# Two buffers for the residual rows h, their norm made at the change of tiles, and the sample tile's loads put in another order

## The reference, cut to what matters

```
proj = rmsnorm(x, norm_mix_w) @ w_in
mix  = concat(window_attention(proj), hgrn2(proj)) @ w_o
h    = x + mix
hn   = h * rsqrt(mean(h*h) + eps) * norm_ffn_w
qry  = hn @ w_q ; sc = qry . sub_keys          # 8 heads x 2 x 128 scores
eidx, gate = top-16 of the 16x16 sums of the two top-16 lists, per head
act  = gelu(peer_u[eidx] . hn)                 # 128 rows of 1024 per token
y    = rmsnorm(h + sum_k gate*act * peer_v[eidx], norm_final_w)
```

## Time and profile before

| what | value |
|---|---|
| time, median of 3 runs | 3365.28 us (3364.44 to 3366.7) |
| the profiled execution | 3362.58 us |
| its span, first to last instruction | 3360.8 us |
| PE, PEld busy | 2938.7 us (87%), 1386.4 us (41%) |
| DVE, ACT, POOL busy | 2104.9 us (63%), 1533.5 us (46%), 2069.1 us (62%) |
| bytes moved by DMA | 1222.63 MB, mean 364 GB/s |
| copies of L1585 (changes of tiles), us | 267.5, 665.8, 1051.4, 1422.6, 1791.1, 2147.1, 2498.4, 2847.1 |
| change to the sample tile's picks (L1582) | 3262.0 us |

### The profile page before, as it was taken

How to read it: one execution, slowest core, us unless ns; L and a number is a source line. 1 busy time by engine, 2 the same in 40 slices (tenths; PEclk the granted TensorE clock), 3 DMA queues, 4 the chain that set the end, 5 groups by cost and what they waited for, 6 DMA issues and landing times.

```text
span 3360.8 us, 31493 instructions
## 1 busy us (share of the span) xinstructions
PE 2938.7 (87%) x8213; PEld 1386.4 (41%) x8213; DVE 2104.9 (63%) x4852; ACT 1533.5 (46%) x4160; POOL 2069.1 (62%) x2162
## 2 busy tenths in 40 slices
PE   8997999979987999789987898789978997689976
PEld 6853544435443444335433443244333442244221
DVE  2465556756575656766585758665776668354694
ACT  3414643357334653367334743475346533263333
POOL 1105565666656666676667766776677667464675
PEclk9998999999999999899999999999989998798999
DMA  8419999999989999999999999999999999899998
GB/s 295 159 51 353 361 386 347 378 410 404 396 319 400 408 390 366 369 410 404 393 329 403 409 410 388 374 409 410 397 361 410 409 404 355 316 379 335 355 353 343
DMA packets 358876, 1222.63 MB, mean 364 GB/s; under 512 B 42747, under 2 KB 65244, under 8 KB 357404
## 3 DMA queue, kind: packets, MB, share of 16 engines
q0 software_dynamic: 308288, 1121.46, 86.0%
q1 hardware_dynamic: 22540, 66.55, 5.3%
q10 hardware_dynamic: 27872, 32.61, 2.9%
HBM read 1195.69 MB, written 25.79 MB: 363 GB/s over the span
## 4 chain that ended last, share of the span: by engine, by line
PE 47%; DMA 17%; DVE 15%; POOL 7%; issue 7%; ACT 6%; SPq 0%; ACTq 0%; DVEq 0%; POOLq 0%
PE ps L1123 24%; DMA rows<-in_peer_v,idx 11%; PE ps L1005 7%; DMA rows<-in_peer_u,idx 6%; PE ps L874 5%; DVE rows L1540 5%; POOL rows L483 4%; PE ps L988 4%; POOL rows L493 4%; PE ps L836 2%; DVE r L1421 1%; DVE r L1422 1%; DVE r L1386 1%; DVE r L1425 1%; DVE r L1381 1%
## 5 line engine op out<-in xcount | busy, mean ns | idle before, releaser
L1123 PE MATMUL ps<-rows,diag 128*128 128x512 f32 (+1 forms) x4224 | 2037.8, 619 | 333.8 <-DMA rows<-in_peer_v,idx 175.3
L1540 DVE CUSTOM_DVE_ANT_0 rows<-rows,ps 128x1024 f32<-128x1024 f32 x1056 | 1261.1, 1217 | 631.2 <-DMA rows<-in_peer_u,idx 628.5
L493 POOL DMA_INDIRECT rows<-in_peer_v,idx x1056 | 1025.7, 971 | 594.0 <-PE ps L1123 376.1
L483 POOL DMA_INDIRECT rows<-in_peer_u,idx x1056 | 1018.4, 964 | 577.7 <-issue 258.9
L1123 PEld LDWEIGHTS ps<-rows,diag 128*128 128x128 f32 (+1 forms) x4224 | 778.0, 193 | 1435.5 <-issue 1114.4
L760 ACT ACTIVATE act_g<-act_g 128x1 f32<-128x1 f32 x1056 | 210.9, 200 | 1070.8 <-DVE act_g L1540 1057.5
L766 ACT ACTIVATE diag<-ident,act_g 128x128 f32<-128x128 f32 x1024 | 411.3, 402 | 400.4 <-PE ps L1123 374.7
L762 ACT ACTIVATE act_g<-act_g,gate 128x1 f32<-128x1 f32 x1056 | 311.0, 295 | 34.3
L1005 PE MATMUL ps<-w_sc,r 128*128 128x512 f32 (+1 forms) x576 | 280.1, 595 | 1.7 <-ACT r L676 1.7
L874 PE MATMUL ps<-rows 128*128 128x416 f32 (+1 forms) x704 | 243.7, 501 | 0.0
L874 PEld LDWEIGHTS ps<-rows 128*128 128x128 f32 x704 | 134.3, 191 | 108.7 <-issue 67.9
(11 more groups left out here) (283 smaller groups left out, 1829.5 us busy)
## 6 DMA issues: line engine op xcount, KB each, us to landing
rows<-in_w_in ACTq DMA_DIRECT2D x42, 512.0 KB, 6.6
rows<-in_peer_u,idx POOLq DMA_INDIRECT x1056, 8.5
rows<-in_peer_v,idx POOLq DMA_INDIRECT x1056, 8.4
r<-proj SPq DMA_DIRECT2D x7, 1344.0 KB, 11.5
proj<-staged ACTq DMA_DIRECT2D x44, 192.0 KB, 7.2
w_sc<-in_w_q_t SPq DMA_DIRECT2D x8, 1024.0 KB, 8.8
rows<-in_w_in POOLq DMA_DIRECT2D x14, 512.0 KB, 3.9
w_o<-in_w_in POOLq DMA_DIRECT2D x10, 512.0 KB, 6.9
```

The lines of the kernel that those rows point to most:

```text
L483: nc.gpsimd.indirect_dma_start(ring[:, slot, :], None, a["peer_u"], bass.IndirectOffsetOnAxis(ap=idx[g % 2][:, k:k + 1], axis=0), engine_s ...
L493: nc.gpsimd.indirect_dma_start(ring[:, slot, :], None, a["peer_v"], bass.IndirectOffsetOnAxis(ap=idx[g % 2][:, k:k + 1], axis=0), engine_s ...
L1123: last = nc.tensor.matmul(Y[j][0:m, :], diag[:, n % DIAGS, 0:m], ring[:, slot, 512 * j:512 * (j + 1)], start=(k == 0), stop=(k == steps_of ...
L1540: V.tensor_tensor_reduce(ring[:, slot, :], ring[:, slot, :], hn_u, 1.0, 0.0, ALU.mult, ALU.add, col).then_inc(S["dots"], 1)
```

## The change

`hx` and `hn` are replaced by `resid[0]` and `resid[1]`; tile t keeps its h in `resid[t % 2]` until its y is stored from there. The DRAM copy of h and its loads are gone.

The front no longer makes `hn`. PE transposes h itself at q = 86. At q = 87 DVE multiplies the transposed rows by `norm_ffn` (a column per partition, `w_ffn_t`, loaded once at the start with elements of 4 bytes) and makes the reciprocal root. ACT applies the root as a scale of its copy of the scores. At the change of tiles, one DVE instruction writes h * rstd * norm_ffn into `hn_u`. For it, `norm_ffn` is loaded into the first half of `r2` as soon as the candidates there are dead (`cand_done`, q = 126), and `norm_final` into the second half at the same time; before, it was loaded after `topk_done`.

Of the sample tile's loads, the copies of the caches between DRAM tensors go to the start of the program, the two cache loads to the period before (after `mix_attn` of tile 7), and `proj_s`, `s_mask`, `s_onehot` and two stores ahead of the y store of tile 6. Only the keys `k_t` (now before the store of `k_win_prompt`) and x_sample stay behind it.

```diff
-        hn = sb("hn", [P, D])
-        hx = sb("hx", [P, D])
+        resid = [sb(f"resid{n}", [P, D]) for n in range(2)]
...
+            sp.dma_start(w_ffn_t, a["norm_ffn"][0, :].rearrange("(c p) -> p c", p=P), allow_slow_non_contiguous=True).then_inc(S["consts_in"], 16)
...
             def load_sample(f):
 
+                sp.dma_start(spj, proj_s[:, 0:CHUNKS - 1, :]).then_inc(S["proj_in"], 16)
+                sp.dma_start(s_mask, a["s_mask"]).then_inc(S["caches_in"], 16)
+                sp.dma_start(s_oh, a["s_onehot"]).then_inc(S["caches_in"], 16)
                 sp.dma_start(a["v_win_prompt"], v_n[:, 1, :]).then_inc(S["out_kv"], 16)
                 sp.dma_start(a["state_prompt"], state[:, :, :]).then_inc(S["out_kv"], 16)
+
+            def load_sample_k(f):
+
                 sp.wait_ge(S["k7_kept"], 1)
+                sp.dma_start(k_t[:, 1, 0:NS], proj_s[:, CHUNKS - 1, :]).then_inc(S["proj_in"], 16)
                 sp.dma_start(a["k_win_prompt"], r3[:, 896:1024]).then_inc(S["out_kv"], 16)
...
                 if f is not None:
                     load_front(f)
+                    if is_sample(f):
+                        load_sample(f)
                     finish(w)
                     if is_sample(f):
-                        load_sample(f)
-                    if f:
-                        sp.wait_ge(S["hn_ready"], f)
-                    sp.dma_start(hx[0:ntok(f), :], a["x_sample"] if is_sample(f) else x_tiles[f]).then_inc(S["x_in"], 16)
+                        load_sample_k(f)
+                    sp.dma_start(resid[f % 2][0:ntok(f), :], a["x_sample"] if is_sample(f) else x_tiles[f]).then_inc(S["x_in"], 16)
+                    if f == TILES - 1:
+                        sp.wait_ge(S["mix_attn"], f + 1)
+                        load_caches()
                     if is_sample(f):
                         sample_caches(f)
-                    sp.wait_ge(S["h_ready"], f + 1)
-                    h_at = h_dram[SEQ:TOK, :] if is_sample(f) else h_tiles[f]
-                    sp.dma_start(h_at, hx[0:ntok(f), :]).then_inc(S["h_stored"], 16)
-                    sp.wait_ge(S["h_stored"], 16 * f + 16)
+                    sp.wait_ge(S["cand_done"], f + 1)
+                    sp.dma_start(w_ffn, a["norm_ffn"]).then_inc(S["w_ffn_in"], 16)
+                    sp.dma_start(w_fin, a["norm_final"]).then_inc(S["w_fin_in"], 16)
...
                         act.wait_ge(S["sc_mm"], 4 * f + g + 1)
+                        act.wait_ge(S["rstd_ready"], f + 1)
                         nc.scalar.activation(sc[0:n, 4 * g:4 * g + 4, :], F[SCORE_BANK[g]][0:n, :].rearrange("p (c t) -> p c t", c=4),
-                                             ACT.Copy).then_inc(S["sc_kept"], 1)
+                                             ACT.Copy, scale=rstd[0:n, :]).then_inc(S["sc_kept"], 1)
...
                 if q == 87:
+                    dve.wait_ge(S["h_turned"], f + 1)
...
+                    for j in range(2):
+                        last = V.tensor_tensor(hn_t[:, 4 * j:4 * j + 4, 0:n],
+                                               F[j][:, 0:4 * n].rearrange("p (c t) -> p c t", c=4),
+                                               w_ffn_t[:, 4 * j:4 * j + 4].unsqueeze(2).to_broadcast([P, 4, n]), ALU.mult)
+                    last.then_inc(S["h_t_kept"], 1)
                     dve.wait_ge(S["ssq_root"], f + 1)
-                    dve.wait_ge(S["w_ffn_in"], 16 * f + 16)
-                    mark(V.reciprocal(rstd[0:n, :], rstd[0:n, :]))
-                    settle()
-                    V.scalar_tensor_tensor(hn[0:n, :], hx[0:n, :], rstd[0:n, :], hn[0:n, :], ALU.mult, ALU.mult)\
-                        .then_inc(S["hn_ready"], 1)
-                    dve.wait_ge(S["hn_ready"], f + 1)
+                    V.reciprocal(rstd[0:n, :], rstd[0:n, :]).then_inc(S["rstd_ready"], 1)
...
                     else:
-                        V.tensor_copy(hn_u, hn[:, :]).then_inc(S["hn_taken"], 1)
-                        dve.wait_ge(S["hn_taken"], f + 1)
+                        mark(V.scalar_tensor_tensor(hn_u, resid[f % 2][:, :], rstd, w_ffn, ALU.mult, ALU.mult))
+                    settle()
```

More of the change, by code:

```diff
@@ L68 @@
 S_OFF = (C_G + 4 - 1) * NS
+S_NEXT = S_OFF + D + NS
 PASS1 = 2 * P
@@ L197, in build @@
         idx = [sb(f"idx{n}", [P, PICKS], I32) for n in range(2)]
-        small = sb("small", [P, 192])
+        small = sb("small", [P, 200])
         ps = ctx.enter_context(nc.psum_tensor("ps", [P, 8, 512], F32))
@@ L212, in build @@
         w_mix = vec(DC)
+        w_ffn_t = vec(DC)
         mix_scale = vec(DC)
@@ L223, in build @@
         staged_s = vec(NS)
-        assert taken[0] <= 192
+        assert taken[0] <= 200
         names = """consts_in w_o_in w_q_in x_a0 x_a1 masks_in masks_kept a_root a_scaled a_turned a_kept w_a0 w_a1 w_a2 w_a3 w_b0 w_b1
@@ L283, in build @@
                     5: (xn_first, 0), 6: (xn_first, P), 7: (xn_first, 2 * P)}
-        table = hn[0:BUCKETS + 1, :].rearrange("p (h q) -> p h q", h=HEADS)
-        bucket_of = hx[0:BUCKETS + 1, 0:SKEW]
+        table = resid[1][0:BUCKETS + 1, :].rearrange("p (h q) -> p h q", h=HEADS)
+        bucket_of = resid[0][0:BUCKETS + 1, 0:SKEW]
         replicated = [r2[:, 0:4 * SKEW], bias[:, 0:4 * SKEW]]
-        w_fin = r2[:, D:2 * D]
+        w_ffn, w_fin = r2[:, 0:D], r2[:, D:2 * D]
         kc_t = bias[:, 0:D]
@@ L295, in build @@
         s_probs_t = [r2[:, D + NS + c * P:D + NS + (c + 1) * P] if c < 7 else
[L296 to L300, removed]
+                     r1[:, S_NEXT + 652 + (c - 7) * P:S_NEXT + 652 + (c - 6) * P] for c in range(9)]
+        s_mask = r1[:, S_OFF:S_NEXT]
+        s_bias = r1[:, S_NEXT:S_NEXT + 264].rearrange("p (g j) -> p g j", g=KV)
+        s_oh = r1[:, S_NEXT + 264:S_NEXT + 396]
+        s_tab = r1[:, S_NEXT + 396:S_NEXT + 652]
         s_nat = r1[0:NS, S_OFF:S_OFF + D]
@@ L370, in finish @@
                     sp.wait_ge(S["y_ready"], w + 1)
-                    sp.dma_start(a["y_sample"] if is_sample(w) else y_tiles[w], hx[0:ntok(w), :]).then_inc(S["y_out"], 16)
+                    sp.dma_start(a["y_sample"] if is_sample(w) else y_tiles[w], resid[w % 2][0:ntok(w), :]).then_inc(S["y_out"], 16)
                     sp.wait_ge(S["y_out"], 16 * w + 16)
@@ L411, in load_sample @@
                 sp.dma_start(vc, a["cache_v"].rearrange("b j x -> j b x")).then_inc(S["caches_in"], 16)
[L412 to L416, removed]
             def sample_caches(f):
@@ L440, in sample_caches @@
                     sp.wait_ge(S[f"st_out{b % 3}"], 16 * (b // 3 + 1))
+            for out_name, in_name in (("k_win_sample", "cache_k"), ("v_win_sample", "cache_v")):
+                sp.dma_start(a[out_name][:, 0:WINDOW - DEC_T, :], a[in_name][:, DEC_T:WINDOW, :])\
+                  .then_inc(S["cache_out"], 16)
             for p in periods:
@@ L666, in front @@
                     act.wait_ge(S["h_ready"], f + 1)
-                    own.mark(nc.scalar.activation(r2[0:n, 0:D], hx[0:n, :], ACT.Square, accum_out=ssq[0:n, :]))
+                    own.mark(nc.scalar.activation(r2[0:n, 0:D], resid[f % 2][0:n, :], ACT.Square, accum_out=ssq[0:n, :]))
                     own.settle()
@@ L670, in front @@
                       .then_inc(S["ssq_root"], 1)
[L671 to L678, removed]
                 for g in range(4):
@@ L793, in _ @@
                         act.wait_ge(S["y_taken"], w + 1)
-                        own.mark(nc.scalar.activation(r2[0:m, 0:D], hx[0:m, :], ACT.Square, accum_out=ssq_y[0:m, :]))
+                        own.mark(nc.scalar.activation(r2[0:m, 0:D], resid[w % 2][0:m, :], ACT.Square, accum_out=ssq_y[0:m, :]))
                         own.settle()
@@ L991, in front @@
                         last.then_inc(S["h_mm"], 1)
-                if q == 88:
-                    pe.wait_ge(S["hn_ready"], f + 1)
-                    turn(F[0], hn[:, 0:512], 4, n)
-                    turn(F[1], hn[:, 512:1024], 4, n).then_inc(S["hn_turned"], 1)
+                if q == 86:
+                    pe.wait_ge(S["h_ready"], f + 1)
+                    turn(F[0], resid[f % 2][:, 0:512], 4, n)
+                    turn(F[1], resid[f % 2][:, 512:1024], 4, n).then_inc(S["h_turned"], 1)
                 if 90 <= q < 114:
@@ L1372, in front @@
                     settle()
+                    dve.wait_ge(S["cand_done"], f + 1)
                     for j in range(2):
```

56 lines of the change are left out of this document (22 added, 34 removed).

## The result

| what | before | after |
|---|---|---|
| median of the runs on one chip, us | 3365.91 (4 runs) | 3330.36 (4 runs, 3324.65 to 3335.46) |
| the profiled execution, us | 3362.58 | 3335.46 |
| its span, us | 3360.8 | 3333.7 |
| bytes moved by DMA | 1222.63 MB | 1214.90 MB |
| changes of tiles, us | (table above) | 265.9, 664.1, 1046.7, 1416.3, 1781.2, 2132.8, 2481.5, 2834.05; sample 3237.16 |

The ratio is 0.9894, 95% interval 0.9877 to 0.9912: faster, by 35.6 us in the medians and by 27.1 us from one profile to the other. The forecast was 3338 us, range 3318 to 3354.

The account below looks back on a forecast made before the run. DMA bounds the first and last stages, PE the projection and scores, DVE the top-16 stage; a chain of waits delays the sample tile. Terms sum to -27.3 us, from the median 3365.28 to 3338 us, range 3318 to 3354.

Parts of the forecast that it names:

- Sample stall: Start of the sample tile: only the keys stay behind the y store, so PE gets on at 2875.8, -16.3 us.
- Rival 4: Start of the sample tile: another late thing ends PE's wait, so the -16.3 goes; 3354 us, chance 0.08.
- Sample and cache loads moved: Loads moved into DMA-bound places: sample loads and stores at topk_done of tile 7 +3.1 us, cache loads in period 6 +2.6.
- The norms at `cand_done`: norm_ffn and norm_final leave DMA-bound places for the stage where DVE is the limit: -15 us, bounds 0 and -17.9.
- rival 1: Only the sample tile gains; bytes moved to cand_done cost there what they saved; 3353 us, chance 0.17.
- rival 3: At cand_done the burst of two loads starves DVE of u rows, +41 us; 3379 us, chance 0.05.
- h out and back: h's store and load, 17.9 us of traffic in the stage where PE is full: valued at 0, bounds 0 and -17.9.
- rival 2: Every byte counts, h's 1 MB beside the full PE too; 3317 us, chance 0.15.
- Transpose two picks earlier: PE before the scores gains 0.25 us a tile, -2 us for 8 tiles, bounds 0 and -7.
- The change of tiles: One DVE instruction of 1285 ns replaces a copy of 1228 ns: +0.7 us, with rounding +1.
- Tile 0: Norm of tile 0, which nothing covers: scores start near 188.6 instead of 190.31, -1.7 us, bounds 0 and -5.
- The start: Load of w_ffn_t, 1,024 elements of 4 bytes, may land late for DVE: +1 us, bounds 0 and +6.

Follow-up runs that it names:

- The whole reordering: Changed kernel with the sample tile's loads and the copies between DRAM tensors put back in their old place: 3337.86 us, 7.4 us above the changed kernel.
- the repeat: The changed kernel run again with no edit, giving its second profile: median 3330.48 us, ratio 0.9896, profiled execution 3331.51 us.
- the kernel with late norms: Changed kernel with norm_ffn and norm_final loaded at topk_done instead of cand_done: 3352.6 us, ratio 0.9968, 22.1 us above the changed kernel.
- the added stores: Changed kernel plus 14 stores of 512 KB behind the keys, at h_ready or at cand_done: 3506.02, 3505.29, 3504.64 us on the third chip, changed kernel 3492.15.
- With the keys early: Changed kernel with the sample tile's keys loaded ahead of the y store of tile 6: 3316.41 us, ratio 0.9861, 14.1 us under the changed kernel.

## Why the prediction was right

The mechanism held for the two large terms. The sum of -27.3 us was made against the profiled execution, and from that to the profiled one after it is -27.1; that these agree to 0.2 us is luck. The medians differ by 35.6, as the profiled run of before was faster than its other runs and that of after the slowest of its four, and the second profile of the changed kernel is 31.1 under the one before. Term by term:

- *Sample stall, -16.3.* PE's wait ends 16.0 us sooner, by the chain that was forecast. But `h_ready` of the sample tile comes only 11.4 us sooner behind the change (245.9 against 257.3), and period 7 is 11.9 us shorter (403.1 against 415.0), not 16; see the last section. Rival 4, that the stall stays, is refuted.
- *Sample and cache loads moved, +5.7.* In period 6 the stage to `h_ready` is 189.8 us, before 187.4, although norm_ffn left it; the last is 23.7, before 22.1, although norm_final left it. With 1.28 added for each, the two groups of loads cost 3.6 and 2.9 us, forecast 2.6 and 3.1. cache_v, for which the prediction had left room up to twice 2.6, took 26.0 us to land there and not 14.2. The whole reordering was measured as 7.4, forecast 10.6.
- *The norms at `cand_done`, -15.* Right in kind, and a little too small. The last stage is 9.8 us shorter over five periods in the profile after (8.8 in the repeat), where five loads at 1.28 are 6.4, and the first 5.1 (7.5), again against 6.4. The direct measurement is 1.23 us a load, close to the 1.28 by rate. I counted 14 loads where there are 15 (norm_final of the sample tile too): 15 x 1.23 = 18.4, just above the bound of 17.9 that I gave. I had doubted whether the fit into 2.8 us of slack was tight; rival 1 hung on that, and rival 3 on starved dots. Both are refuted: that stage is 116.8 us over five periods before, with the norms in it, and with them late.
- *h out and back, 0.* The stage in which they stood took 601.0 us before and 600.6 in each of three profiles without them, where ten transfers at 1.28 would be 12.8. What the kernel with late norms gains and loses against before in the other stages is one load each: -8.0 in the first (6.4 for norm_ffn's going), +5.8 in the last (6.4 for its coming). The medians say the same: that kernel is 11.7 us under the one before on one chip, of which the reordering is 7.4 and tile 0 is 1.6. That leaves 2.7 us, or some 5 if tile 0's late pair is charged, with about 5 of uncertainty, for the h traffic and all else; rival 2 wants 17.9 for the h traffic alone. That the bytes lay beside PE is read from profiles of kernels that differ in more than this, and the added stores ran only where DMA was slower; a run of them on the first chip is missing.
- *Transpose two picks earlier, -2.* 0.1 us a tile and not 0.25: as argued, the next pick waits for ACT's diagonal, which the change leaves as it was.
- *The change of tiles, +1.* Eight instructions of 1.294 us in place of 1.228: +0.5, and the rest unseen.
- *Tile 0, -1.7.* The scores start at 188.74, forecast 188.6, before 190.31.
- *The start, +1.* 0.

With the measured parts (-7.4, -18.4, -1.6 for tile 0) the sum is -27.4; the median gives -33.8 on the chip where they were measured. Each part is a difference of medians whose intervals are about 5 us each way, so the 6 us between may be scatter; no run explains them. The forecast came near in part because the reordering gave less than its 10.6 us while the norms gave more than their 15.

## What to carry to other kernels

Where gathers keep DMA full, price every transfer by its bytes at the rate of that stage and look for a stage with another limit to put it in: 512 KB cost about 1.2 us in one stage and nothing measurable 23 us earlier. Of a load that is waited for, ask what it is queued behind: taking the keys from behind a store's completion was worth 14 us, and cost no byte. Such a place should be tried on more than one chip: on the one that moved 377 GB/s and not 406, 14 added stores cost some 13 us by the medians wherever they stood.

## What was not expected of the hardware

*PE's clock in the sample tile's states.* The 16.0 us won at the stall were 11.4 at `h_ready`. Both kernels below have the same stall end (29.0 and 28.8 us behind the change), and a stage with the sample's states, in which PE waits some us at L1086. Windows of 10 us there, in the changed kernel:

```profile
3004.00:3014.00 10.00, 6.74 (x28) 4.53 (x28) 2.65 (x7) 0.90 (x3) 3.49 (x4) 0.67 0.85 287
3014.00:3024.00 10.00, 10.00 (x30) 7.18 (x30) 3.31 (x10) 0.90 (x3) 1.87 (x2) 0.50 0.63 204
3024.00:3034.00 10.00, 10.00 (x24) 5.92 (x23) 5.05 (x13) 1.39 (x5) 1.87 (x2) 0.50 0.58 201
```

And with the norms late, at the same distance from the change:

```profile
3019.00:3029.00 10.00, 9.23 (x35) 6.27 (x36) 2.80 (x8) 0.90 (x3) 2.97 (x4) 0.65 0.70 207
3029.00:3039.00 10.00, 10.00 (x24) 5.66 (x24) 4.75 (x13) 1.40 (x5) 1.87 (x2) 0.52 0.85 305
3039.00:3049.00 10.00, 10.00 (x38) 5.64 (x37) 6.77 (x14) 4.21 (x14) 5.99 (x7) 0.97 0.77 261
```

PE is busy all of the time at a granted clock of 0.50, that is 1.2 GHz, for 20 us in the one and for about 10 in the other. What that costs is in PE's own rows of the changed kernel, before and in that stretch:

```profile
2988.88 1.15 PE L1090 MATMUL ps<-r 32*128 32x128 f32 x8
2989.96 1.99 PE L1112 MATMUL ps<-rows,diag 128*128 128x512 f32 x4
2996.51 1.25 PE L1086 MATMUL ps<-bias 128*128 128x4 f32 x8 [4.56 <-issue]
...
3012.24 1.84 PE L1086 MATMUL ps<-bias,r 128*128 128x4 f32 x8 [2.80 <-issue]
...
3021.22 2.07 PE L1090 MATMUL ps<-r 32*128 32x128 f32 x8
3023.23 3.78 PE L1112 MATMUL ps<-rows,diag 128*128 128x512 f32 x4
```

The same pick takes 3.78 us and not 1.99, behind waits of 4.56 and 2.80 us. The stage to `h_ready` is 6.0 us longer in the changed kernel than with the norms late (245.9 against 239.9). The clock can be a part of that, and not the whole. If PE's busy time is weighted with the granted clock over ten such windows, from 140 to 240 us behind the change, the changed kernel does 76.2 us of full-speed work and the other 81.4. Of these 5.2 us, 2.8 are waits (9.0 us idle against 6.2) and 2.5 the clock (14.9 us lost against 12.4), by this estimate. With the keys early the clock is 1.00 from 3012 on, 180 us behind the change, and the same estimate gives 9.4 us lost to it (ten windows, 130 to 230 us behind the change), against 15.3 in its neighbour (140 to 240). So that kernel's period 7 could lose 19.9 us (381.8 against 401.6) where the stall had 13.4. That the clock is a cause was not tested by a run of its own.

*Chips.* The kernel before ran 4.6% and 5.3% longer on the other two chips (3519.25 and 3542.11 against 3364.3). The Trainium skill (page "DMA: Bandwidth & Descriptors", section "Where 436 GB/s comes from") puts the limit for HBM to SBUF at about 358 GB/s for a core, and "Perfetto Trace Analysis", section "Roofline", says that a core may pull more while the other of its pair is idle. The 406 to 409 GB/s of the first two profiles, before and after, agree with the second statement and not with the first alone. The fullest rows of the third chip above (377 and 382 GB/s, both at share 0.99) lie between 358 and 406. No run here shows what else, if anything, used that chip's memory.
